# The last two heads' queries and the side projection, moved from one block behind the first unit of gathered rows to six pieces behind the first six

## The reference

```python
def peer_ffn(h, w_q, sub_keys, expert_u, expert_v):      # per block of 128 tokens
    q = (hb @ w_q).reshape(n, PEER_HEADS, 2, PEER_HALF)  # 8 heads, 2 halves of 128
    s = jnp.einsum('nhcd,hckd->nhck', q, sub_keys)       # 128 keys per half
    sc, ix = lax.top_k(s, PEER_TOPK)                     # 16 best of each half
    cand = sc[:, :, 0, :, None] + sc[:, :, 1, None, :]
    cidx = ix[:, :, 0, :, None] * PEER_N_KEYS + ix[:, :, 1, None, :]
    top, pos = lax.top_k(cand.reshape(n, PEER_HEADS, PEER_TOPK * PEER_TOPK), PEER_TOPK)
    eidx = jnp.take_along_axis(cidx.reshape(n, PEER_HEADS, -1), pos, axis=-1)
    gate = jax.nn.softmax(top, axis=-1)
    act = jax.nn.gelu(jnp.einsum('nhed,nd->nhe', expert_u[eidx], hb), approximate=False)
    return jnp.einsum('nhe,nhed->nd', (gate * act), expert_v[eidx])

x = x + peer_ffn(rmsnorm(x, g_ffn[i]), ...)
x = x + (p[i] @ w_ple_proj[i]) * jax.nn.sigmoid(rmsnorm(x, g_ple[i]) @ w_ple_gate[i])
```

## Time and profile before

| | |
|---|---|
| runs: median, lowest, highest | 2450.94, 2449.79, 2454.59 us |
| the profiled execution | 2459.51 us, span 2457.8 us |
| busy over the span: PE, ACT, DVE, POOL | 86%, 32%, 49%, 28% |
| gathers, share of 16 DMA engines over the span | 268.53 MB, 29.2% |
| chain that ended last | PE 68%, POOL 10%, issue 6%, DVE 6%, DMA 4% |

### The profile page before, as it was taken

One profiled execution on the slowest core, in us unless ns is written; L12 is line 12 of the kernel. 1 busy time (PEld: TensorE's weight loads), 2 busy tenths in 40 slices (PEclk: granted clock), 3 DMA queues, 4 the chain that ended last, 5 costly groups with the idle time before them and its releaser, 6 DMA issues.

```text
span 2457.8 us, 34543 instructions
## 1 busy us (share of the span) xinstructions
PE 2106.7 (86%) x13812; PEld 1680.0 (68%) x13812; DVE 1200.8 (49%) x2250; ACT 787.8 (32%) x1321; POOL 678.1 (28%) x702
## 2 busy tenths in 40 slices
PE   7999989999999999999995999986867667667677
PEld 7999878998999878999773887872422222223235
DVE  5455426445455434453336443285465566566432
ACT  4444535335344533443133223121222121212122
POOL 0000010000001000000006321047477777777770
PEclk9999999999999959999996997998888989878999
DMA  8554316554554305553420100579599999999990
GB/s 293 190 191 129 119 52 206 188 171 155 188 183 142 121 1 169 184 191 116 124 76 17 36 20 19 173 258 396 201 374 342 360 373 366 346 373 364 358 371 31
DMA packets 253787, 489.56 MB, mean 199 GB/s; under 512 B 13872, under 2 KB 173136, under 8 KB 253536
## 3 DMA queue, kind: packets, MB, share of 16 engines
q0 software_dynamic: 73888, 268.53, 29.2%
q1 hardware_dynamic: 176016, 214.32, 26.9%
q10 hardware_dynamic: 3760, 5.02, 0.6%
HBM read 486.74 MB, written 1.05 MB: 198 GB/s over the span
## 4 chain that ended last, share of the span: by engine, by line
PE 68%; POOL 10%; issue 6%; DVE 6%; DMA 4%; ACT 3%; another core or an unknown queue 1%; DVEq 0%; ACTq 0%; POOLq 0%
PE bank L704 67%; POOL arena_sb L2356 8%; POOL con_sb L2356 2%; DMA con_sb<-peer_v,arena_sb 1%; DMA arena_sb<-peer_u,arena_sb 1%; DVE parts_sb L1756 1%; DMA arena_sb<-peer_v,arena_sb 1%; DVE sq_sb L1775 1%; PE bank L851 1%; DVE xl_sb L1779 1%; ACT parts_sb L1384 1%; DVE arena_sb L2023 0%; DVE arena_sb L2103 0%; DMA xT_sb<-xT 0%
## 5 line engine op out<-in xcount | busy, mean ns | idle before, releaser
L704 PE MATMUL bank<-arena_sb 64*64 64x64 f32 (+8 forms) x3704 | 554.9, 338 | 195.2 <-ACT arena_sb L1705 119.3
L704 PE MATMUL bank<-xh_sb,parts_sb 128*128 128x256 f32 x3328 | 608.4, 285 | 19.0 <-DVE xl_sb L1779 11.9
L704 PEld LDWEIGHTS bank<-arena_sb 64*64 64x64 f32 (+4 forms) x3704 | 330.8, 172 | 415.6 <-issue 259.9
L704 PEld LDWEIGHTS bank<-xh_sb,parts_sb 128*128 128x128 f32 x3328 | 515.2, 190 | 29.6 <-issue 19.1
L704 PE MATMUL bank<-xl_sb,parts_sb 128*128 128x256 f32 x1664 | 469.5, 282 | 0.0
L2234 DVE CUSTOM_DVE_ANT_0 sq_sb<-arena_sb 128x1024 f32<-128x1024 f32 x256 | 309.6, 1224 | 265.2 <-DMA arena_sb<-peer_u,arena_sb 249.1
L1756 DVE TENSOR_TENSOR parts_sb<-ring_sb,parts_sb 128x2048 fp32r<-128x2048 f32 x132 | 298.6, 2290 | 192.2 <-ACT parts_sb L1384 192.2
L2356 POOL DMA_INDIRECT arena_sb<-peer_u,arena_sb x256 | 272.1, 1063 | 194.7 <-DVE arena_sb L2204 110.6
L704 PEld LDWEIGHTS bank<-xl_sb,parts_sb 128*128 128x128 f32 x1664 | 316.5, 190 | 0.0
L1384 ACT ACTIVATE parts_sb<-ring_sb 128x2048 fp32r<-128x2048 f32 x132 | 247.9, 1910 | 96.5 <-PE bank L704 95.1
L704 PE MATMUL bank<-xn_sb,ring_sb 128*128 128x256 f32 (+1 forms) x1200 | 271.1, 386 | 8.4 <-DVE xn_sb L1775 4.9
(11 more groups left out here) (246 smaller groups left out, 1718.6 us busy)
## 6 DMA issues: line engine op xcount, KB each, us to landing
ring_sb<-ffn_w_gate SPq DMA_DIRECT2D x44, 1024.0 KB, 5.5
ring_sb<-ffn_w_up SPq DMA_DIRECT2D x44, 1024.0 KB, 6.6
ring_sb<-ffn_w_down SPq DMA_DIRECT2D x44, 1024.0 KB, 4.9
ring_sb<-w_in SPq DMA_DIRECT2D x17, 1024.0 KB, 5.3
ring_sb<-w_in_ab SPq DMA_DIRECT2D x12, 1024.0 KB, 5.2
ring_sb<-w_out SPq DMA_DIRECT2D x12, 1024.0 KB, 5.1
ring_sb<-w_in_cd SPq DMA_DIRECT2D x12, 1024.0 KB, 5.4
ring_sb<-peer_w_q SPq DMA_DIRECT2D x8, 1024.0 KB, 5.4
```

The source lines that it names most:

```text
L704: return pe.matmul(dst, lhsT, rhs, start=start, stop=stop_, skip_group_check=loose)
```

## The change

The function `queries(h)` (both halves of a head, then its scores) becomes `query(m)` (one half; the scores follow the second half), and `projection()` takes four of its eight groups at a time. A table says which piece stands behind which unit. ACT's copies are cut in the same way. No instruction is added or taken away on any engine, and the lines of the new file lie 1 to 10 further on.

```diff
+        LATE = {0: ("query", 12), 1: ("query", 13), 2: ("query", 14), 3: ("query", 15), 4: ("ple", 0), 5: ("ple", 4)}
...
                 for u in range(16):
                     weighted_rows(u)
-                    if u == 0:
-                        for h in range(FIRST_HEADS, 8):
-                            queries(h)
-                        projection()
+                    if u in LATE:
+                        kind, m = LATE[u]
+                        if kind == "query":
+                            query(m)
+                        else:
+                            projection(m)
...
-                def projection():
+                def projection(first):
                     k = at["pp"]
-                    have(k)
-                    pe.wait_ge(S("p_loaded"), 16)
-                    for m in range(8):
+                    if first == 0:
+                        have(k)
+                        pe.wait_ge(S("p_loaded"), 16)
+                    for m in range(first, first + 4):
...
-                    if u == 0:
-                        for m in range(FIRST_HEADS, 8):
-                            head_out(m)
-                        for m in range(8):
-                            b = take(act, ("pp", m))
-                            give(act.activation(PLE[:, m, :], b[:, 0:T], ACT.Copy), ("pp", m))
+                    if u in LATE:
+                        kind, first = LATE[u]
+                        if kind == "query":
+                            query_out(first)
+                        else:
+                            for m in range(first, first + 4):
+                                b = take(act, ("pp", m))
+                                give(act.activation(PLE[:, m, :], b[:, 0:T], ACT.Copy), ("pp", m))
```

More of the change, by code:

```diff
@@ L1252, in scores, with query @@
                     fill_end(ins, ("sc", h))
-                def queries(h):
+                def query(m):
+                    h, c = m // 2, m % 2
                     k = at["wq"] + h
-                    have(k)
[L1258 to L1268, removed]
+                    if c == 0:
+                        have(k)
+                    b = fill_begin(pe, ("pq", m))
+                    for kk in range(KC):
+                        if m == 0:
+                            pe.wait_ge(xn_ready, KC * 7 + kk + 1)
+                        ins = mm(b[:, 0:T], slot(k, KC, 256)[:, kk, c * P : (c + 1) * P], xn[:, kk, :], kk == 0, kk == KC - 1)
+                        if kk == 0:
+                            release(ins)
+                    fill_end(ins, ("pq", m))
+                    if c == 1:
+                        owed[0] += 1
+                        scores(h)
                 def tokens():
@@ L1286, in projection @@
                             ins = mm(b[:, 0:T], slot(k, 2, 1024)[:, kk, m * P : (m + 1) * P], PIN[:, kk, :], kk == 0, kk == 1)
-                            if m + kk == 0:
+                            if m + kk == first:
                                 release(ins)
                         fill_end(ins, ("pp", m))
-                    owed[0] += 1
+                    owed[0] += first == 4
                 def weighted_rows(u):
@@ L1318, in experts @@
                 pe.wait_ge(S("keys_loaded"), 16)
-                for h in range(FIRST_HEADS):
-                    queries(h)
-                    if h == 0:
+                for m in range(2 * FIRST_HEADS):
+                    query(m)
+                    if m == 1:
                         tokens()
@@ L1674, in experts, with query_out @@
             def experts():
[L1675 to L1679, removed]
+                def query_out(m):
+                    b = take(act, ("pq", m))
+                    give(act.activation(QP[:, m % 4, :], b[:, 0:T], ACT.Copy), ("pq", m))
+                    if m % 2 == 0:
+                        return
+                    h = m // 2
                     b = take(act, ("sc", h))
@@ L1683, in head_out @@
                     give(act.activation(SC[1][:, 2 * h : 2 * h + 2, :], sc[:, 1, :, :], ACT.Copy), ("sc", h))
-                for h in range(FIRST_HEADS):
-                    head_out(h)
-                    if h == 0:
+                for m in range(2 * FIRST_HEADS):
+                    query_out(m)
+                    if m == 1:
                         for j in range(4):
```

## The result

Over eight runs of each kernel on one chip the kernel after has a median of 2440.97 us (2431.47 to 2453.64) and the kernel before 2453.28 us (2446.18 to 2464.99). The ratio is 0.995, with a 95% interval of 0.9928 to 0.9973: a gain of 12.3 us.

The account below looks back on a forecast made before the run. The expert layer was taken to run at the pace of POOL's issues and the transfers, with one hole. Terms -19.8 + 3.4 + 2.9 + 0 = -13.5 from 2450.94 gave 2437.4, forecast as 2438 us, range 2424 to 2446.

Parts of the forecast that it names:

- The hole at unit 1: POOL's 30.9 us wait for PE at unit 1's gather shrinks to 10.8: -19.8 us (-30.6 to -19.8).
- the hold: 13.0 us between PE's end of head 6's first half and ACT's copy of it, cause unknown; assumed to stay.
- hold gone: Upper end at unit 1: ACT's copy comes without the 13.0 us delay, so the whole 30.6 us go.
- Rival A: The 13.0 us delay is real in the runs and goes with the block: gain 24.3 us, 2420 to 2431; chance 0.19.
- The third reading: Profile's 8.6 us over the runs belongs to the hold; the runs' 17.6 us hole goes whole: -11.3, or 2439.6 us.
- Regained by before: Before's faster pace from unit 2 on, its rings filled during the hole, is lost: +3.4 us (0 to 3.4).
- The load: The fourth `w_ple_gate` slot's 1.05 MB, moved during the hole before, now goes between gathers: +2.9 us (0 to 2.9).
- The five pieces: Later query and projection halves behind units 1 to 5 fit PE's idle time: 0 us, bound +5.
- Rival C: Late PE releases recur at five unit boundaries; slower from 7.6 us each, 2478 us at 13.0 each; chance 0.08.
- Rival B: Transfers give the gain back through a slower pace in the first six units: no change, 2446 to 2455; chance 0.11.

Follow-up runs that it names:

- ACT first: The kernel before with only ACT's tables, exponential and gelu of unit 1 moved ahead of the block's copies; ratio to before 0.9969.
- head by head: Against after: a whole head behind unit 0, another behind unit 1, projection behind units 2 and 3; as fast as after, profiled execution 2456.04 us.
- Light: After with one matmul instead of eight in each of four late query halves, queries incomplete; two chips, mean ratio to before 0.9920.
- four halves in one block: Against after: all four query halves behind unit 0, projection behind units 4 and 5; before's time, within 3.2 us of gain and 7.1 of loss.
- triple: After with the matmuls of every late piece done three times; 0.71% slower than before, 1.21% (30 us) slower than after.
- before again: The kernel before, unchanged, timed and traced a second time; ratio 1.0022 to before.
- after again: The kernel after, unchanged, timed and traced again beside before; 2437.25 us, ratio 0.995.
- seven and eight ahead: After with seven or all eight heads' queries ahead of the gathered rows; seven 2.1 us faster than after on one chip, eight 0.9956 to before.

## Why the prediction was right

The forecast was 2438 us and a gain of 13.5; the runs gave 12.3 and a median 3 us above the forecast. Of these 3, 2.3 are the base: I took the 2450.94 of three runs, and eight have 2453.28. The mechanism of the hole is shown: POOL's wait, DVE's wait for the exponential and the empty stretch are gone together, and ACT's order alone brings about 7.6 of the 12.3 us. That the number came so close is in part luck, as the first step says. By its own steps:

*The hole at unit 1, -19.8 (-30.6 to -19.8).* The place and the mechanism were right; the hold was read wrongly. I kept it at the same place in both kernels. In all three traces of after ACT copies that half within 0.04 us of its end on PE, and "hold gone" holds to the microsecond: unit 1's first row was to come at about 1713, and it came at 1706.39 in an execution whose gathers began 7.7 us earlier (1609.34 for 1617.02), so at 1714.1. From unit 0 to unit 1 the two pairs of traces save 77.3 - 48.0 = 29.3 and 70.4 - 48.0 = 22.4 us, where "hold gone" had said 30.6. The range held it in the trace; the value I took did not.

Why does the sum still fit the runs? The stage (from the first gather to the end) is 840.8 and 845.4 us in the traces of before, and 820.4, 822.2 and 821.4 in those of after: 21.8 us between the means. But the two profiled executions of before, 2459.51 and 2460.95, stood 6.2 and 7.7 us above the medians of before on their chips, and after's three 9.5 and 0.4 below and 2.9 above theirs, 2.3 below on average. 21.8 - 7.0 - 2.3 = 12.5, which is the runs' gain. So the profiled pairs differ by more than ordinary ones. An ordinary execution of before may have less hold than the two that were profiled, but no trace shows one, and this subtraction doesn't say in which part of the kernel their excess lies. Against it stands that the second was only 2.4 above the median of its own twelve runs (2458.50). By keeping the 13.0 in both kernels I took it out of the difference. For an event that an ordinary run doesn't have, that gives the right number, but it was not my reason: I expected the hold to stay, and it went. That is the luck in the -19.8.

*Rival A.* The stages of the traces saved 21.8 us, near its 24.3, which the interval of the runs (6.6 to 17.7 us) excludes. Its reason, that the long block makes the hold, is refuted as a rule: in ACT first PE has the whole block and every copy but one (0.15) starts within 0.04 us of its matmuls, and head by head has a hold of 10.5 us behind a block of one head.

*The third reading, -11.3.* It has the nearest number and an unfounded reason. The 8.6 us between profile and runs are no effect of the profiler: after's profiled execution is below its median. It is the scatter of executions.

*Regained by before, +3.4.* The traces agree: from unit 1 to unit 2 before takes 43.0 and 44.2 us, after 46.7, 46.2 and 46.0, 2.7 more on average.

*The load, +2.9.* The load moved as I said; its price is not resolved. The queue of plain loads moves nothing from 1717 to 1748 any more, and the megabyte goes between gathers; these rows (packets, MB, share) are of 1740 to 1760 and of 1760 to 1790:

```profile
q1 hardware_dynamic: 323, 0.33, 4.8%
```

```profile
q1 hardware_dynamic: 717, 0.72, 6.9%
```

From unit 2 to unit 14 after takes 560.9, 561.9 and 561.4, before 556.3 and 560.5: 3.0 more on average, for this term and the next together, where before's own two lie 4.2 apart.

*The five pieces, 0 (bound +5).* The queries ran at the full clock: 3.62 us behind units 0 to 3 of the profiled execution, as the row had it. The spare between gelu and weights came out at 0.6, 2.6, -1.2, 0.4 and 4.5 us for units 2 to 6, where I had worked out 0.5, 1.7, 1.4, 2.1 and 1.6. Only unit 4 overran, and its 1.22 us stayed inside POOL's slack of 3.4. Light's 3 us less by unit 4 leave a small cost possible, inside the bound; the 7.6 (give or take 6) of its runs are more than I can place.

*Rival C.* Its mechanism exists. In the second trace of after the last copy behind unit 4 starts 6.7 us behind the end of its matmuls (1886.24 + 3.62 = 1889.86), and POOL waited 4.8; in light's second POOL waited 11.2:

```profile
1886.24 3.62 PE L705 MATMUL bank<-arena_sb,ring_sb 128*128 128x256 f32 x16
...
1896.57 0.38 ACT L1721 ACTIVATE arena_sb<-bank 128x256 f32<-128x256 f32 x1 [5.26 <-remote]
```

I had asked for it at every boundary, from 7.6 us each; it comes now and then, and after is not slower in any of three comparisons.

*Rival B* is refuted for after: it needed over 48 us for a unit, and from unit 1 to unit 6 the three traces have 47.2, 46.8 and 46.7 on average.

Still open: what makes a release of PE late, why four halves in one block gained nothing, where half of triple's 30 us goes, and where the rest of light's 8 us comes from.

## What to carry to other kernels

Where an engine's program has a side job ahead of the small operations that feed the critical stage, look at the order on every engine that the job passes, not only on the one that computes it: here ACT's copies stood ahead of an exponential, and moving that exponential and the gelu, with their table loads, ahead of them brought about 7.6 of the 12.3 us. Cut such a job to pieces shorter than the idle time that the fed engine has anyway (pieces of 3.6 us into 10 cost a few us in all at most, six pieces of 10.5 us lost 30). And before a stall in one trace is priced, set that execution's time beside the median of the runs: an unexplained part of the stall may be an accident that the typical run doesn't have.

## What the runs showed of the hardware

PE's releases can come late in a stage that fills the DMA engines. Thirteen traces have a half query (in light a single matmul of it) behind unit 0; in eleven ACT copied it within 0.7 us of its end on PE, in two it was 13.0 and 10.5 us late. Others fell on later pieces: 5.0 in before again, 5.1 and 12.3 to 16.8 in light's two, 6.1 in head by head, 6.7 in after again, 7.8 in triple. The semaphore itself moves late: in before its update stands at 1719.88, 0.03 us ahead of ACT's copy. The DMA engines were 0.99 to 1.03 busy in the stretches where they fell, the trace names "remote" as what ended ACT's wait, and the granted clock falls to 0.50, which is 1.2 GHz, in or just behind each, after PE's idle time. Such busy engines are the rule in this stage, though, and most releases in it are on time, so the share alone is not the cause. The traces of seven and eight ahead have none over 1.4 us. One rival can be looked up: the packets that the profile calls instruction. One of 8 KB starts inside three of the holds (at 1714.7 in before and in head by head, at 1890.2 in light's second), but none inside triple's, and in after one starts at 1700.2 with no hold there. So they don't explain all of them, and the cause stays open.

Two executions of one kernel begin the stage at different times, although everything ahead is the same: 1609.3, 1612.9 and 1622.3 us in after's three traces, whose stages then agree within 1.8 us. Over all fourteen traces it is 1605.2 to 1623.3. Of a difference between two single executions of this kernel, 13 us and more can thus lie where nothing was changed.
